# Banded attention's 36 steps dealt out 3, 1, 1 and 2 to a weight slot instead of 2 throughout, and each score matmul waiting for its own PSUM bank alone

## The chip, the cores and the metric

One core of a Trainium2 chip runs the whole program as one launch. The metric is the device time of an execution in microseconds (us), the median of three runs. Five engines work side by side, each through its own list of instructions in order: TensorE (PE in the profile, its weight loads PEld), VectorE (DVE), ScalarE (ACT), GpSimd (POOL) and SyncE (SP), which issues the transfers. They meet at semaphores.

## The reference, cut to what matters

Two transformer blocks over 512 tokens of width 1024, all in float32. The first block projects the normed input by one matrix into the parts of three branches and their gates. The change lies where branch A, attention in a band of 128 positions, runs beside the projections of branch C and of gate A:

```python
qa = apply_rope(rms_norm(qa.reshape(B, S, 8, 64), qn_a[l]), cos, sin)      # 8 query heads, 2 key heads
out_a = window_attention(qa, ka, va, sink_a[l])      # blocks of 128 queries, their own and the neighbouring keys
qc = apply_rope(rms_norm(qc.reshape(B, S, 8, 64), qn_c[l]), cos, sin)
kc = apply_rope(rms_norm(kc.reshape(B, S, 8, 64), kn_c[l]), cos, sin)
out_c = diff_attention(qc, kc, vc, lam)
g = sigmoid(gate_logits)
merged = g[0] * (out_a @ w_oa) + g[1] * (out_b @ w_ob) + g[2] * (out_c @ w_oc)
```

## The kernel before

**Groups and slots.** Every big product is a group (`groups()`): `qc`, `kc`, `vc` are the projections of branch C, `gA0` and `gA1` the two halves of gate A, `bA0` and `bA1` the product of branch A's output with `w_oa`. A group's weights come in slots of 128 x 1024 numbers, two of its eight k-tiles to a slot, so each of `qc`, `kc`, `vc`, `gA0`, `gA1` has four slots. ACT copies a slot into `whi`, and POOL (for `qc`, `kc`, `vc`) or DVE (for the rest) takes the rounding error into `wlo`. TensorE then does four blocks of six matmuls for a slot, one block for each of the PSUM banks 0 to 3. At a group's last slot each block is complete and is read by `evac`.

**Steps beside the slots.** Attention is written as a generator, `window()`, in each engine's program. It has 36 steps, and `Flow.pump` takes one. `slots()` deals the steps out by `rate`: at rate 2 a step stands behind the second and the fourth block of a slot, at rate 3 one behind each of the second, third and fourth, at rate 1 one behind the fourth. A step is pumped at the same place of each engine's program. With u the step's number, TensorE does these things in step u: `turn(u - 3)`, the transposes of a finished softmax into bank 6; for even u `scores(u)`, the scores of heads u and u + 1 into banks 4 and 5; for odd u `values(u - 5)`, two products into bank 7. DVE does `lowest(u)`, which reads the score out of bank 4 + u % 2 into the tile `T8` with its row minimum (L1089), and `shares(u - 1)`, which sums, inverts and scales (L1095, L1097, L1099). ACT copies the transposes out and takes the exponentials. Every eighth step has a block of 128 queries finished: ACT's `high` (L1637) writes `oahi` and DVE's `low` (L1103) `oalo`, which `bA0` multiplies.

**Rotary embedding.** The four blocks of `qc` and of `kc` need more work: a copy and a square on ACT (L1602, L1608), a sum on DVE (L1038), an inverse root on POOL (L2037, L2039), then `products` on DVE (L1043, L1051), `turn` on POOL (L2047, L2048), `sums` on DVE (L1056). `Flow.later` sets these behind a count of slots: `products` of blocks 0 and 1 at the end of the group's last slot; at the end of the next slot their `sums` and the `products` of blocks 2 and 3; one slot later the `sums` of those. `rotary(r, b)` on TensorE transposes block b into bank 4 + b % 2. Blocks 0 and 1 are transposed at the end of the second slot behind the group, just before the step pumped there, blocks 2 and 3 one slot later. They use the banks of the scores, so they wait too until `lowest` has read what the last `scores` wrote there: `free[b]` holds that condition, and `take(b)` waits for it.

Of the kernel before, what the change touches and what calls it, by code (L numbers as in the profile page):

```python
# [151 lines left out]
def build(nc, d, out):  # L152
# [76 lines left out]
    qcT = sb("qcT", AR + 107.5, [128, 4, S])  # L229
    kcT = sb("kcT", AR + 115.5, [128, 4, S])  # L230
    vc = sb("vc", AR + 123.5, [128, 4, 512])
# [144 lines left out]
    def tensor_program(t):  # L376
# [4 lines left out]
        def take(b):  # L381

            for s, n in free[b]:
                w.wait_ge(s, n)

        def mm(o, l, r, first, last):
            return t.matmul(o, l, r, start=first, stop=last)  # L387
# [4 lines left out]
        def group(name, act, ready, freed, rate=1, more=False, beside=None, last=True):  # L392
            first, n_s, n, mode = PLACE[name]
            for s, b, end in slots(flow, name, rate, nothing):
                i, bank = first + s, BANK[name] + b
                h = i % HL
                if b == 0:
                    w.wait_ge(lo_done[h], i // HL + 1)
                if s == 0 and not more:
                    take(bank)  # L400
                if s == 1 and beside:
                    beside(b, bank)
                for kk in range(2):
                    k = 2 * s + kk
                    ready(k, b)
                    ahi, alo = act(k)
                    if mode == "tok":
                        c0, c1 = kk * n, kk * n + n
                        rows = slice(b * 128, b * 128 + 128)
                        o = ps[bank][:, 0:n]  # L410
                        mm(o, ahi[:, rows], whi[h][:, c0:c1], s == 0 and kk == 0 and not more, False)
                        mm(o, ahi[:, rows], wlo[h][:, c0:c1], False, False)
                        op = mm(o, alo[:, rows], whi[h][:, c0:c1], False, last and end and kk == 1)
                    else:
                        c0 = kk * n + b * 128
                        o = ps[bank][:]
                        mm(o, whi[h][:, c0:c0 + 128], ahi, s == 0 and kk == 0 and not more, False)
                        mm(o, whi[h][:, c0:c0 + 128], alo, False, False)
                        op = mm(o, wlo[h][:, c0:c0 + 128], ahi, False, last and end and kk == 1)
                if end:  # L420
                    op.then_inc(blocks, 1)
                    reader = freed(b)
                    free[bank] = [reader] if reader else []
                elif b == (4 if mode == "tok" else n // 128) - 1:
                    op.then_inc(slot_read[h], 1)
# [4 lines left out]
        def h_ready(n):  # L430
            return (lambda k, b: w.wait_ge(e_lo, 8 * n - 8 + k + 1)) if n else (lambda k, b: w.wait_ge(n_lo, k + 1))
# [128 lines left out]
        def rotary_group(name, r, nj, rate=1):  # L560
            def freed(b):
                flow.later(3 + b // 2 if r else 5, lambda: rotary(r, b, nj))
                return r_c, 4 * r + b + 1
            group(name, hT, h_ready(0), freed, rate)

        def window():
            w.wait_ge(r_e, 8)

            def scores(u):

                n, h = w_units[u]
                k0, wd, _ = span_a(n)
                take(4)
                take(5)
                for i in range(2):
                    base = 64 * i
                    mm(ps[4 + i][:, 0:wd], qaT[base:base + 64, h, n * 128:(n + 1) * 128],
                       kaT[base:base + 64, 0, k0 * 128:k0 * 128 + wd], True, True).then_inc(a_qk, 1)
                    free[4 + i] = [(a_mx, u + i + 1)]

            def turn(u):
                wd = span_a(w_units[u][0])[1]
                w.wait_ge(a_nm, 3 * u + 3)
                take(6)
                for k in range(wd // 128):
                    op = across(6, k, T8[u % 4][:, k * 128:(k + 1) * 128])
                op.then_inc(a_tr, 1)
                free[6] = [(a_ev, u + 1)]

            def values(u):  # L590

                n, h = w_units[u]
                k0, wd, _ = span_a(n)
                w.wait_ge(a_ev, u + 2)
                if h == 0:
                    take(7)
                for k in range(wd // 128):
                    for i in range(2):
                        op = mm(ps[7][64 * i:64 * i + 64, h * 128:(h + 1) * 128], va[:, k0 + k, 64 * i:64 * i + 64],
                                PT[(u + i) % 4][:, k * 128:(k + 1) * 128], k == 0, k == wd // 128 - 1)  # L600
                        if k == wd // 128 - 1:
                            op.then_inc(a_pv, 1)
                if h == 3:
                    free[7] = [(oa_lo, n + 1)]

            for u in range(36):
                if 3 <= u < 35:
                    turn(u - 3)
                if u < 32 and u % 2 == 0:
                    scores(u)  # L610
                if u >= 5 and u % 2:
                    values(u - 5)
                yield
# [180 lines left out]
            group("bB%d" % half, lambda k: (obhi[:, k, :], oblo[:, k, :]), lambda k, b: w.wait_ge(ob_lo, 4),  # L794
                  lambda b: (b_v, 4 * half + b + 1), 2)
        flow.beside.append(window())
        rotary_group("qc", 2, 4, 2)
        rotary_group("kc", 3, 4, 2)
        group("vc", hT, h_ready(0), lambda b: (vc_c, b + 1), 2)
        flow.flush()  # L800
        for half in range(2):
            group("gA%d" % half, hT, h_ready(0), lambda b: (g_t, 8 + 4 * half + b + 1), 2)
# [50 lines left out]
    def vector_program(v):  # L853
# [13 lines left out]
        def group(name, evac, rate=1):  # L867
            for _, b, end in slots(flow, name, rate, split):
                if end:
                    evac(b, ps[BANK[name] + b], DONE[name] + b + 1)  # L870
# [160 lines left out]
        def rotary(r, n_heads):  # L1031
            def evac(b, p, done):
                q, wd = 4 * r + b, 64 * n_heads
                r_, q0, q1 = (rk[:, b, :] if r == 1 else raw[b])[:, 0:wd], tp[b % 2][:, 0:wd], tq[b % 2][:, 0:wd]
                s0 = 64 + 16 * b
                ss = st[:, s0:s0 + n_heads]
                w.wait_ge(r_q, q + 1)
                v.tensor_reduce(ss, heads(q0, n_heads), AX.X, ALU.add).then_inc(r_s, 1)  # L1038
                cg = rt[:, 2 * r, b, :].unsqueeze(1).to_broadcast([128, n_heads, 64])

                def scale():
                    w.wait_ge(r_r, 2 * q + 2)
                    v.tensor_tensor(heads(r_, n_heads), heads(r_, n_heads), ss.unsqueeze(2).to_broadcast([128, n_heads, 64]),  # L1043
                                    ALU.mult).then_inc(r_x, 1)

                def times_cos():
                    w.wait_ge(r_x, q + 1)
                    w.wait_ge(r_tab, 13)
                    if b < 2:
                        w.wait_ge(r_s, q + 3)  # L1050
                    v.tensor_tensor(heads(q0, n_heads), heads(r_, n_heads), cg, ALU.mult).then_inc(r_m, 1)  # L1051

                def add():
                    w.wait_ge(r_m, q + 1)
                    w.wait_ge(r_g, q + 1)
                    v.tensor_tensor(r_, q0, q1, ALU.add).then_inc(r_a, 1)  # L1056

                waiting.append((scale, times_cos, add))
                if b % 2:
                    two = tuple(waiting)  # L1060
                    waiting.clear()

                    def products():
                        two[0][0]()
                        two[1][0]()
                        two[0][1]()
                        two[1][1]()

                    def sums():
                        two[0][2]()  # L1070
                        two[1][2]()

                    flow.later(1 + b // 2, products)
                    flow.later(2 + b // 2, sums)
            return evac
# [338 lines left out]
        for half in range(2):  # L1414
            group("bB%d" % half, branch(0, half), 2)
        flow.beside.append(window())
        group("qc", rotary(2, 8), 2)
        group("kc", rotary(3, 8), 2)
        group("vc", none, 2)
        flow.flush()  # L1420
        for half in range(2):
            group("gA%d" % half, none, 2)
# [55 lines left out]
    def scalar_program(a):  # L1478
# [413 lines left out]
        for half in range(2):  # L1892
            group("bB%d" % half, none, 2)
        flow.beside.append(window())
        group("qc", rotary(2, 8, qcT), 2)
        group("kc", rotary(3, 8, kcT), 2)
        group("vc", values, 2)
        flow.flush()
        for half in range(2):
            group("gA%d" % half, gates(1, half), 2)  # L1900
# [45 lines left out]
    def gpsimd_program(g):  # L1946
# [248 lines left out]
        for half in range(2):  # L2195
            group("bB%d" % half, none, 2)
        flow.beside.append(iter(range(36)))
        group("qc", rotary(2, 8), 2)
        group("kc", rotary(3, 8), 2)
        group("vc", none, 2)  # L2200
        flow.flush()
        for half in range(2):
            group("gA%d" % half, none, 2)
# [248 lines left out]
```

## Time and profile before

| | |
|---|---|
| median of 3 runs | 1698.64 us (1698.61 to 1698.65) |
| the profiled execution, its own time | 1700.36 us |
| its span in the trace | 1698.5 us |
| TensorE busy | 1633.2 us, 96% of the span |
| VectorE, ScalarE, GpSimd busy | 883.5, 645.4 and 366.1 us |
| mean granted TensorE clock | 0.991 of full speed |
| the 36 steps and the groups beside them | from 318.24 us to 468.5 us; `bA0` begins at 479.53 us |

The span is shorter than the execution by what lies around it, 1.9 us. A busy TensorE is not one at its peak: the ends of matmuls are modelled, and the distance between two starts tells what one takes.

### The profile page before, as it was taken

What the parts mean: (1) busy time and instruction counts of PE and PEld (TensorE: products, weight loads), DVE (VectorE), ACT (ScalarE), POOL (GpSimd) and SP (SyncE); (2) the same over time, 40 slices, a digit from 0 to 9 for tenths busy, and PEclk for the clock granted to TensorE, in tenths of its full rate; (3) what the DMA queues carried; (4) which work ended last, traced back from release to release, by engine and by line L of the source; (5) the groups of instructions that cost most, each with busy time, mean ns of one, the idle gap of its engine ahead of it and who ended that gap; (6) DMA issues with size and microseconds to landing.
All of it is one profiled execution on the core that took longest, in us unless ns stands there. A gap on an engine that the chain in (4) does not pass through costs nothing.

```text
span 1698.5 us, 19241 instructions
## 1 busy us (share of the span) xinstructions
PE 1633.2 (96%) x7582; PEld 1292.9 (76%) x7582; DVE 883.5 (52%) x1401; ACT 645.4 (38%) x1106; POOL 366.1 (22%) x318
## 2 busy tenths in 40 slices
PE   5999998988999999999999999998999999999998
PEld 3566787766767788888888887775788888888886
DVE  5446555366357555444343324587564767777222
ACT  4332223355445433333322212466563444444222
POOL 3444214364012116111110205033202400000000
PEclk9999998999999999999999999999999999999999
DMA  6121112211221323233333322321102232332322
GB/s 231 51 74 37 50 55 75 87 57 56 75 63 50 112 88 98 92 95 99 99 100 94 94 98 70 112 63 38 44 7 76 86 98 90 97 99 87 124 88 73
DMA packets 39221, 139.51 MB, mean 82 GB/s; under 512 B 4331, under 2 KB 4971, under 8 KB 38940
## 3 DMA queue, kind: packets, MB, share of 16 engines
q1 hardware_dynamic: 39132, 138.29, 25.3%
q8 instruction: 60, 0.98, 0.2%
q14 instruction: 29, 0.24, 0.0%
HBM read 136.14 MB, written 2.10 MB: 81 GB/s over the span
## 4 chain that ended last, share of the span: by engine, by line
PE 83%; DVE 6%; POOL 5%; ACT 3%; issue 3%; DMA 1%; SPq 0%; POOLq 0%; DVEq 0%; ACTq 0%
PE ps L387 80%; PE ps L390 3%; POOL sqs L2105 2%; POOL sqt L2103 1%; DVE raw L1056 1%; ACT whi L1489 1%; DVE W L1307 0%; DVE wlo L863 0%; DVE T L1089 0%; DMA wraw<-in_ws 0%; DMA x<-in_x 0%; POOL Lb L2158 0%; DVE tp L1051 0%; DVE sd L962 0%; DVE raw L1043 0%
## 5 line engine op out<-in xcount | busy, mean ns | idle before, releaser
L863 DVE TENSOR_TENSOR wlo<-wraw,whi 128x1024 fp32r<-128x1024 f32 (+2 forms) x220 | 271.8, 1240 | 442.7 <-ACT whi L1489 442.0
L387 PE MATMUL ps<-hThi,whi 128*128 128x512 f32 x1128 | 455.0, 403 | 1.6 <-DVE skT L1394 0.9
L387 PE MATMUL ps<-hThi,wlo 128*128 128x512 f32 x1128 | 441.5, 391 | 0.0
L387 PE MATMUL ps<-hTlo,whi 128*128 128x512 f32 x1128 | 440.9, 391 | 0.0
L1489 ACT ACTIVATE whi<-wraw 128x1024 fp32r<-128x1024 f32 (+2 forms) x244 | 251.9, 1037 | 481.9 <-PE ps L387 467.9
L387 PEld LDWEIGHTS ps<-hThi,whi 128*128 128x128 f32 x1128 | 212.9, 189 | 57.5 <-issue 16.2
L387 PEld LDWEIGHTS ps<-hTlo,whi 128*128 128x128 f32 x1128 | 213.0, 189 | 45.5 <-issue 3.6
L387 PEld LDWEIGHTS ps<-hThi,wlo 128*128 128x128 f32 x1128 | 212.6, 188 | 45.3
L387 PE MATMUL ps<-whi,hThi 128*128 128x512 f32 (+1 forms) x224 | 90.1, 402 | 6.8 <-DVE wlo L863 6.8
L387 PE MATMUL ps<-whi,hTlo 128*128 128x512 f32 (+1 forms) x224 | 85.9, 383 | 0.0
L387 PE MATMUL ps<-wlo,hThi 128*128 128x512 f32 (+1 forms) x224 | 85.8, 383 | 0.0
L2242 POOL TENSOR_TENSOR small<-small,vec 128x1 f32<-128x1 f32 x4 | 2.2, 540 | 355.0 <-DVE small L1469 355.0
L1956 POOL TENSOR_TENSOR wlo<-wraw,whi 128x1024 fp32r<-128x1024 f32 x24 | 59.1, 2463 | 85.5 <-ACT whi L1489 85.5
L2122 POOL TENSOR_TENSOR ft<-ft,R 128x512 f32<-128x512 f32 x22 | 27.9, 1290 | 199.1 <-ACT ft L1729 199.1
L387 PE MATMUL ps<-whi,achi 128*128 128x512 f32 x176 | 69.2, 393 | 0.0
L387 PE MATMUL ps<-wlo,achi 128*128 128x512 f32 x176 | 68.5, 389 | 0.0
L387 PE MATMUL ps<-whi,aclo 128*128 128x512 f32 x176 | 68.5, 389 | 0.0
L387 PE MATMUL ps<-achi,whi 128*128 128x512 f32 x176 | 68.5, 389 | 0.0
L387 PE MATMUL ps<-aclo,whi 128*128 128x512 f32 x176 | 68.5, 389 | 0.0
L387 PE MATMUL ps<-achi,wlo 128*128 128x512 f32 x176 | 68.5, 389 | 0.0
L387 PEld LDWEIGHTS ps<-whi,hThi 128*128 128x128 f32 x224 | 43.7, 195 | 21.3 <-issue 7.7
L1740 ACT ACTIVATE ft<-vt,vec 128x512 f32<-128x512 f32 x44 | 34.9, 813 | 51.0 <-DVE vt L1245 51.0
(323 smaller groups left out, 2605.7 us busy)
## 6 DMA issues: line engine op xcount, KB each, us to landing
wraw<-in_ws SPq DMA_DIRECT2D x236, 512.0 KB, 3.5
x<-in_x SPq DMA_DIRECT2D x4, 512.0 KB, 7.5
x<-in_x SPq DMA_DIRECT2D x1, 2048.0 KB, 8.4
out<-ys SPq DMA_DIRECT2D x8, 256.0 KB, 2.2
dec<-in_dec SPq DMA_DIRECT2D x1, 1024.0 KB, 15.9
wraw<-in_ws SPq DMA_DIRECT2D x4, 256.0 KB, 2.6
vec<-in_vec SPq DMA_DIRECT2D x1, 788.0 KB, 4.7
w<-in_w SPq DMA_DIRECT2D x1, 512.0 KB, 14.3
```

The source lines that it names most:

```text
L387: return t.matmul(o, l, r, start=first, stop=last)
L390: return t.transpose(ps[b][:, c * 128:(c + 1) * 128], src, ident)
L863: v.tensor_tensor(wlo[h][:, 0:width(i)], wraw[h][:, 0:width(i)], whi[h][:, 0:width(i)].bitcast(F32), ALU.subtract).then_inc(lo_done[h], 1)
L1056: v.tensor_tensor(r_, q0, q1, ALU.add).then_inc(r_a, 1)
L1489: a.activation(whi[h][:, 0:width(i)], wraw[h][:, 0:width(i)], ACT.Copy).then_inc(hi_done[h], 1)
L1740: a.activation(ft[i][:], vt[q % 4][:], ACT.Identity, bias=col("cb2", c), scale=col("cw2", 88 + c)).then_inc(v_a, 1)
L1956: g.tensor_tensor(wlo[h][:, 0:width(i)], wraw[h][:, 0:width(i)], whi[h][:, 0:width(i)].bitcast(F32), ALU.subtract).then_inc(lo_done[h], 1)
L2103: g.tensor_tensor(sqt[:], xT[:, f, :], xT[:, f, :], ALU.mult).then_inc(p_acc, 1)
L2105: g.tensor_tensor(sqs[:], sqs[:], sqt[:], ALU.add).then_inc(p_acc, 1)
L2122: g.tensor_tensor(t[:], t[:], R1[:], ALU.mult).then_inc(u_sr, 1)
L2242: g.tensor_tensor(small[:, 8 + b:9 + b], small[:, 4 + b:5 + b], col("mhalf"), ALU.pow).then_inc(n_rs, 1)
```

## The change

`groups` `qc`, `kc` and `vc` are run at rates 3, 1 and 1 in place of 2, 2 and 2, in the programs of all four compute engines. The gates keep rate 2. So 12, 4 and 4 steps stand beside the three groups where there were 8, 8 and 8, and 16 are left for the 16 places of the two gates, where there were 12. And `scores` no longer waits for both banks before its two matmuls: each matmul waits for its own bank. No instruction is added or removed but waits. The diff; the three hunks left out make the same change of rates in VectorE's, ACT's and POOL's programs:

```diff
@@ -570,10 +570,9 @@
 
                 n, h = w_units[u]
                 k0, wd, _ = span_a(n)
-                take(4)
-                take(5)
                 for i in range(2):
                     base = 64 * i
+                    take(4 + i)
                     mm(ps[4 + i][:, 0:wd], qaT[base:base + 64, h, n * 128:(n + 1) * 128],
                        kaT[base:base + 64, 0, k0 * 128:k0 * 128 + wd], True, True).then_inc(a_qk, 1)
                     free[4 + i] = [(a_mx, u + i + 1)]
@@ -794,9 +793,9 @@
             group("bB%d" % half, lambda k: (obhi[:, k, :], oblo[:, k, :]), lambda k, b: w.wait_ge(ob_lo, 4),
                   lambda b: (b_v, 4 * half + b + 1), 2)
         flow.beside.append(window())
-        rotary_group("qc", 2, 4, 2)
-        rotary_group("kc", 3, 4, 2)
-        group("vc", hT, h_ready(0), lambda b: (vc_c, b + 1), 2)
+        rotary_group("qc", 2, 4, 3)
+        rotary_group("kc", 3, 4, 1)
+        group("vc", hT, h_ready(0), lambda b: (vc_c, b + 1), 1)
         flow.flush()
         for half in range(2):
             group("gA%d" % half, hT, h_ready(0), lambda b: (g_t, 8 + 4 * half + b + 1), 2)
```

The two places that matter below, as the built programs have them. First VectorE behind the end of the group `kc`. `raw` and `tp` are the tiles of the rotary embedding, `T8` those of the attention's scores, `st` holds columns of one number per row. Before:

```order
L1089 ISA T8_0_123,st_132<-ps4,maskA_131,small_61 128x384
L1089 ISA st_132 128x1
L1095 TENSOR_TENSOR st_132<-st_132 128x1
L1097 RECIPROCAL st_132<-st_132 128x1
L1099 TENSOR_SCALAR T8_3_126<-T8_3_126,st_132 128x384
L1056 TENSOR_TENSOR raw0_111<-tp0_116,tp2_118 128x512
L1056 TENSOR_TENSOR raw1_112<-tp1_117,tq1_119 128x512
L1043 TENSOR_TENSOR raw2_113<-raw2_113,st_132 128x512
L1043 TENSOR_TENSOR raw3_114<-raw3_114,st_132 128x512
L1051 TENSOR_TENSOR tp0_116<-raw2_113,rt_110 128x512
L1051 TENSOR_TENSOR tp1_117<-raw3_114,rt_110 128x512
L1089 ISA T8_1_124,st_132<-ps5,maskA_131,small_61 128x384
```

After:

```order
L1088 ISA T8_3_126,st_132<-ps5,maskA_131,small_61 128x384
L1088 ISA st_132 128x1
L1094 TENSOR_TENSOR st_132<-st_132 128x1
L1096 RECIPROCAL st_132<-st_132 128x1
L1098 TENSOR_SCALAR T8_2_125<-T8_2_125,st_132 128x384
L1055 TENSOR_TENSOR raw0_111<-tp0_116,tp2_118 128x512
L1055 TENSOR_TENSOR raw1_112<-tp1_117,tq1_119 128x512
L1042 TENSOR_TENSOR raw2_113<-raw2_113,st_132 128x512
L1042 TENSOR_TENSOR raw3_114<-raw3_114,st_132 128x512
L1050 TENSOR_TENSOR tp0_116<-raw2_113,rt_110 128x512
L1050 TENSOR_TENSOR tp1_117<-raw3_114,rt_110 128x512
L1088 ISA T8_0_123,st_132<-ps4,maskA_131,small_61 128x384
```

Between the `products` of the first two blocks and their `sums` (`raw0`, `raw1`) stands one step less; and the step behind the second `products` is an even one, whose score is in bank 4 (step 16), where it was an odd one with bank 5 (step 17).

Second TensorE where `gA1` ends (`ps3`, the last block) and `bA0` begins (`oahi`, `oalo`). Before:

```order
L387 MATMUL ps3<-hThi_49,wlo0_57 128x512
L387 MATMUL ps3<-hThi_49,whi0_54 128x512
L387 MATMUL ps3<-hTlo_50,whi0_54 128x512
L387 MATMUL ps3<-hThi_49,wlo0_57 128x512
L387 MATMUL ps0<-oahi_136,whi1_55 128x512
L387 MATMUL ps0<-oalo_137,whi1_55 128x512
```

After:

```order
L387 MATMUL ps3<-hThi_49,wlo0_57 128x512
L387 MATMUL ps7<-PT2_129,va_122 64x128
L387 MATMUL ps7<-PT3_130,va_122 64x128
L387 MATMUL ps7<-PT2_129,va_122 64x128
L387 MATMUL ps7<-PT3_130,va_122 64x128
L387 MATMUL ps0<-oahi_136,whi1_55 128x512
L387 MATMUL ps0<-oalo_137,whi1_55 128x512
```

The last `values` of the attention (`PT`, `va`), from which `oahi` and `oalo` are made, moved from eight blocks of matmuls ahead of `bA0` to directly in front of it.

## Rows read from the trace of the kernel before

**Rows 1.** The page's busy times.

```profile
PE 1633.2 (96%) x7582; PEld 1292.9 (76%) x7582; DVE 883.5 (52%) x1401; ACT 645.4 (38%) x1106; POOL 366.1 (22%) x318
```

**Rows 2.** TensorE's waits from 312 to 480 us: total, times, longest.

```profile
PE ps L387 <- DVE st L1089: 7.8, 4, 2.9
PE ps L390 <- DVE st L1089: 2.4, 2, 2.0
```

**Rows 3.** Timeline of TensorE, its waits: start, length, instruction, idle time before it.

```profile
348.03 0.92 PE L387 MATMUL ps<-kaT,qaT 64*128 64x384 f32 x4 [1.43 <-DVE st L1089]
...
358.75 0.92 PE L387 MATMUL ps<-kaT,qaT 64*128 64x384 f32 x4 [2.88 <-DVE st L1089]
...
365.04 0.63 PE L390 MATMUL ps<-vec,raw 128*128 128x128 f32 x4 [0.40 <-DVE st L1089]
...
388.22 0.92 PE L387 MATMUL ps<-kaT,qaT 64*128 64x384 f32 x4 [1.04 <-DVE st L1089]
...
398.91 0.92 PE L387 MATMUL ps<-kaT,qaT 64*128 64x384 f32 x4 [2.40 <-DVE st L1089]
...
405.21 0.63 PE L390 MATMUL ps<-vec,raw 128*128 128x128 f32 x4 [2.03 <-DVE st L1089]
```

**Rows 4.** Timeline of TensorE, work of the steps and blocks.

```profile
382.60 0.49 PE L390 MATMUL ps<-vec,T 128*128 128x128 f32 x3
...
391.93 0.49 PE L390 MATMUL ps<-vec,T 128*128 128x128 f32 x3
392.35 0.88 PE L387 MATMUL ps<-PT,va 128*64 128x128 f32 x12
396.02 0.49 PE L390 MATMUL ps<-vec,T 128*128 128x128 f32 x3
```

**Rows 5.** Timeline of TensorE behind the wait of 2.88 us.

```profile
359.97 0.63 PE L387 MATMUL ps<-wlo,hThi 128*128 128x512 f32 x1
...
363.35 0.39 PE L387 MATMUL ps<-whi,hThi 128*128 128x512 f32 x1
...
364.04 0.60 PE L390 MATMUL ps<-vec,raw 128*128 128x128 f32 x4
```

**Rows 6.** Stretches: length, busy PE, PEld, DVE, ACT, POOL, granted clock, DMA.

```profile
284.00:288.00 4.00, 2.24 (x10) 2.24 (x11) 4.00 (x5) 0.52 (x3) 2.29 (x3) 0.50 0.33 69
288.00:292.00 4.00, 4.00 (x23) 4.00 (x22) 2.39 (x5) 2.43 (x11) 1.75 (x4) 0.55 0.76 217
...
396.00:400.00 4.00, 1.60 (x9) 0.82 (x8) 3.81 (x8) 1.20 (x4) 3.49 (x4) 1.00 0.27 107
```

**Rows 7.** Timeline of VectorE behind the end of `kc`.

```profile
384.44 0.69 DVE L1038 TENSOR_REDUCE st<-tp 128x8 f32<-128x512 f32 x1 [0.46 <-ACT tp L1608]
...
398.15 0.60 DVE L1089 CUSTOM_DVE_ANT_0 T<-ps,maskA,small 128x384 f32<-128x384 f32 x1
...
399.07 0.64 DVE L1099 TENSOR_SCALAR T<-T,st 128x384 f32<-128x384 f32 x1
...
400.76 2.57 DVE L1099 TENSOR_SCALAR T<-T,st 128x384 f32<-128x384 f32 x1
403.25 0.68 DVE L1056 TENSOR_TENSOR raw<-tp,tp 128x512 f32<-128x512 f32 x1
```

**Rows 8.** Timeline of POOL over the same stretch.

```profile
379.87 0.20 POOL L2037 TENSOR_SCALAR st<-st 128x8 f32<-128x8 f32 x1
...
388.39 0.72 POOL L2047 TENSOR_TENSOR tp<-raw,rt 128x256 f32<-128x256 f32 x1
...
400.72 2.39 POOL L1956 TENSOR_TENSOR wlo<-wraw,whi 128x1024 fp32r<-128x1024 f32 x1 [1.22 <-ACT whi L1489]
```

**Rows 9.** Timelines of TensorE, ACT and DVE at the last `values`.

```profile
467.89 0.66 PE L387 MATMUL ps<-PT,va 128*64 128x128 f32 x8
...
468.62 0.60 ACT L1637 ACTIVATE oahi<-ps 128x512 fp32r<-128x512 f32 x1 [2.99 <-PE ps L387]
...
469.25 0.69 DVE L1103 TENSOR_TENSOR oalo<-ps,oahi 128x512 fp32r<-128x512 f32 x1 [5.17 <-ACT oahi L1637]
```

More of the change, by code:

```diff
@@ L1416, in vector_program @@
         flow.beside.append(window())
-        group("qc", rotary(2, 8), 2)
-        group("kc", rotary(3, 8), 2)
-        group("vc", none, 2)
+        group("qc", rotary(2, 8), 3)
+        group("kc", rotary(3, 8), 1)
+        group("vc", none, 1)
         flow.flush()
@@ L1894, in scalar_program @@
         flow.beside.append(window())
-        group("qc", rotary(2, 8, qcT), 2)
-        group("kc", rotary(3, 8, kcT), 2)
-        group("vc", values, 2)
+        group("qc", rotary(2, 8, qcT), 3)
+        group("kc", rotary(3, 8, kcT), 1)
+        group("vc", values, 1)
         flow.flush()
@@ L2197, in gpsimd_program @@
         flow.beside.append(iter(range(36)))
-        group("qc", rotary(2, 8), 2)
-        group("kc", rotary(3, 8), 2)
-        group("vc", none, 2)
+        group("qc", rotary(2, 8), 3)
+        group("kc", rotary(3, 8), 1)
+        group("vc", none, 1)
         flow.flush()
```

## The prediction

> **What bounds the kernel now.** The page's busy times come first: TensorE is busy for 96% of the span [rows 1], so time can only be won where it waits or runs slowly. The list of its waits over the stretch with the attention's steps shows few: four at line 387 and two at line 390, 10.2 us, all for VectorE's line 1089, the read of a score [rows 2]. The timeline places them [rows 3]. They come in two bunches of three, one behind the end of `qc` and one behind the end of `kc`: 1.43, 2.88 and 0.40 us, then 1.04, 2.40 and 2.03 us. In each bunch the first two stand in front of scores and the third in front of the rotary transposes of block 1. So it is not the score reads that are slow, but what VectorE has queued in front of them: the rotary work of the group that has just ended. Nothing else in the 36 steps holds TensorE. After the wait of 2.88 us the clock fell: from 359.97 to 363.35 us the starts of eight matmuls stand 0.42 us apart, behind it 0.23 [rows 5], which is the 1.2 GHz level against 2.4. That lost 8 x 0.19 = 1.5 us, but to no effect, since the transposes of block 1 at 365.04 still had to wait 0.40 us for VectorE. What the present order pays in the two bunches is then 10.2 + 1.5 = 11.7 us.
>
> **The change: how late VectorE is.** I count from the transposes behind the last block of the rotary group, 382.60 us for `kc` [rows 4]. POOL begins the four inverse roots at 379.87 and the rotary products at 388.39, 8.5 us later, and it must do the roots of all four blocks first [rows 8]. VectorE's `sums` and second `products` follow these, and only then, at 398.15, comes the score read, done at 398.8, 16.2 us behind the count [rows 7]. In the new order that same place, behind the second `products`, is held by the read of step 12 (in `kc`'s case 16), in bank 4, as the order of VectorE shows. One step less is queued in between, but POOL's part is what the others wait for, so I do not take the 1.3 us of a step off. On the other side the four blocks of `kc` now follow each other with no step between them, so the group ends about 1.3 us earlier against POOL's `wlo` and roots, and in `qc` a step stands between the third and the fourth block, where VectorE and ACT hand work to each other. Each makes VectorE some 1.3 us later against the end of the group: 17.5 us, between 16.2 and 18.
>
> **When TensorE gets there.** From 388.22 to 396.02 TensorE did scores, 12 matmuls, transposes, values and 12 matmuls, 7.8 us [rows 3, 4]. In the new order there stand between the end of the group and the rotary transposes of blocks 0 and 1: two slots of 24 matmuls, but only two steps. That is the 7.8 us, one more `turn` of 0.42 (391.93 to 392.35 [rows 4]) and 24 more matmuls at 0.23 [rows 5], 5.5 us: 13.7 us. Now the scores no longer wait (their readers are through), and the edit of the banks has nothing left to save there; where it acts it lets one matmul of 0.4 us pass, and I cost it at nothing. The wait moves to the transposes of block 0, which need bank 4, so the read that is done at 17.5: 3.8 us, between 2.5 and 4.3. I take 3.6. Behind them queue the transposes of block 1, the step, and all matmuls of the next slot.
>
> **The second wait.** The transposes of block 1 need bank 5, so the odd step's read. On VectorE one `shares`, the two `sums` and the read itself stand in between. By the rows a `shares` is 0.35 us of small work and its scaling, 0.64 us at 399.07 and 2.57 us at 400.76 [rows 7], where POOL had begun a `wlo` of 2.39 us at 400.72 [rows 8]. ACT casts that slot only after the exponential of the first read, so in the new order, with one `shares` fewer, the scaling should be through before POOL starts. Then 0.35 + 0.4 + 1.2 + 0.6 = 2.55 us, less the 0.46 us of block 0's transposes: 2.1 us. If the scaling falls behind POOL it is 4.3. The Trainium skill says why it can (GPSIMD Engine Reference, Specifications): GpSimd shares its SBUF interface with VectorE and contends with VectorE's two-port and two-input instructions; by that rule the sum is the same, it only names which instructions can be caught.
>
> A bunch then costs 3.6 + 2.1 = 5.7 us and the two 11.4, against 11.7: the main edit wins 0.3 us.
>
> **What is new.** (a) In `qc` three steps stand in a slot, two of the distances being one block (6 x 0.23 = 1.4 us). ACT's part of a step with a raw copy and a square of the rotary group is longer than that, so a turn or a score there waits a little: 0.8 us, between 0 and 1.5. (b) The 36 steps now end in the last slot of `gA1`. In front of `bA0` stand the last `values`, ACT's `oahi` and VectorE's `oalo`. Today these are hidden under eight blocks: `values` begins at 467.89, `oahi` at 468.62, `oalo` at 469.25, for 0.69 us [rows 9]. The chain is 2.05 us, of which TensorE works 0.6: a new wait of 1.5 us, with nothing else for it to do, since `bA0`'s first matmul reads them. (c) The clock. TensorE now stands for 3.6 + 2.1 us with only the 0.5 us of block 0's transposes between. After 2.88 us it lost 1.5; at 1.04 and 2.40 us, a slot apart, the clock stayed full through 396 to 400 [rows 6]; after the longest wait of the kernel it stood at 0.50 and 0.55 for 284 to 292 us, with work in all but 1.8 us of it [rows 6], a loss of about 2.9 us. A low stretch of the length of the first (3.4 us), begun about when the transposes come, lies for 2.1 us in the second wait, where it costs nothing, and then costs 0.6; one as after the long wait costs 2.9. Nearer the first: I take 1.15 us for each bunch, 2.3 in all, between 0 and 5.8. And unlike today nothing stands behind that would have waited anyway.
>
> The Trainium skill has a rule that speaks against this change (TensorE: Matmul & The Clock Gate, HAM oscillation): idle gaps of TensorE let its clock fall to half, and the penalty is half of the time at that clock. By it few long gaps are worse than many short ones of the same sum. The rows agree: 1.5 us lost after 2.88 us of wait, nothing after 2.40.
>
> **The sum.** -0.3 + 0.8 + 1.5 + 2.3 = +4.3 us. The profiled execution took 1700.36 us with a span of 1698.5, so it should become 1704.7, the span 1702.8. The median of the runs, 1698.64, stands 1.7 below the profiled time; the same 4.3 us make it 1702.9 us.
>
> **The rivals.** *The clock holds* (or falls only inside the waits): +2.0 us, 1700.6. For it speaks that two waits of 2.40 and 2.03 us in one bunch cost no clock; against it, that now they stand with no slot between. *The chain of VectorE counts its steps and not POOL's roots.* Then the read of the even step is done one step sooner and not 1.3 us later, at 16.2 - 1.6 = 14.6 us, and the first wait is 0.9 us. A bunch costs 3.0 us, the two 6.0, a gain of 5.7, and with 1.5 for `bA0` and no low clock the kernel is 4.2 us faster: 1694.4. It decides from a first wait below about 2 us on. Against it stand POOL's 8.5 us of roots [rows 8]. *The scaling falls behind POOL's `wlo` in both bunches, with the clock low for longer*: 2.2 us more for each bunch, +8.7 us: 1707.3. *Nothing moves*, as the waits are only placed elsewhere and `bA0` waits for nothing: 1698.6; the rows of the last `values` speak against it.
>
> **How the numbers follow.** Chances: the forecast (a low clock in at least one bunch, both waits as above) 0.55; the clock holds 0.18; the chain by steps, faster, 0.10; caught behind POOL 0.12; nothing moves 0.05. A measurement of this kernel can tell about 0.2% (3.4 us). The forecast's own spread, 1701 to 1705, lies with a quarter of its chance below that bound, so slower by over 0.2% has 0.42 + 0.12 = 0.54, within it 0.13 + 0.18 + 0.05 = 0.36, faster 0.10. The range reaches down to 1698.5, taking in the held clock, and up to 1707: it leaves out the faster case and part of the one behind POOL.
>
> **What would show it.** In the trace of the changed kernel: TensorE's waits at line 387 for the score reads (four, 7.8 us) gone or below 1 us each; at line 390 two pairs of about 3.6 and 2.1 us; a wait of about 1.5 us for `oalo` in front of `bA0`; a granted clock of about half for some us behind each pair. The forecast is wrong if the first wait of a pair is under 2 us, if scores still wait for more than a us each, or if the clock stays full over both.

## The result and the profile after

| | before | after |
|---|---|---|
| median of the five runs of each, taken together | 1698.61 us (1696.29 to 1698.65) | 1706.03 us (1704.13 to 1707.84) |
| ratio | | 1.0047, 95% interval 1.0032 to 1.0061 |
| the profiled execution, its own time and span | 1700.36, 1698.5 us | 1704.13, 1702.2 us |
| first score to the first matmul of `bA0` | 318.24 to 479.53: 161.3 us | 315.11 to 483.50: 168.4 us |

The change costs 7.4 us, or 0.47%. The forecast was +4.3 us; 1706.03 us lies in its range, near the upper end. The profiled execution of after was the fastest of its five, and its span is only 3.7 us longer. It started the attention's steps 3.1 us earlier, though nothing ahead of them was changed. The clock was back earlier in this execution, as the windows behind the kernel's longest wait show for after (columns as in [rows 6]):

```profile
280.00:284.00 4.00, 0.06 (x1) 0.06 (x1) 4.00 (x5) 0.00 (x0) 4.00 (x4) 0.52 0.00 0
284.00:288.00 4.00, 4.00 (x23) 4.00 (x24) 4.00 (x5) 1.79 (x8) 0.47 (x1) 0.63 0.46 142
288.00:292.00 4.00, 4.00 (x29) 3.65 (x28) 1.75 (x8) 3.94 (x11) 3.24 (x8) 1.00 0.71 253
```

In [rows 6] the clock was still at 0.50 and 0.55 in the last two of these stretches, with the same work. So executions of one program can differ by some 3 us here, and the two kernels are compared over the stretch in which they differ: 168.4 against 161.3 us, +7.1, which agrees with the medians.

TensorE's busy time is what it was, 1634.3 us against 1633.2 [rows 1], and so are the other engines':

```profile
PE 1634.3 (96%) x7582; PEld 1292.0 (76%) x7582; DVE 881.6 (52%) x1401; ACT 645.5 (38%) x1106; POOL 367.8 (22%) x318
```

TensorE's waits from 312 to 490 us in after (total, times, longest), the counterpart of [rows 2]:

```profile
PE ps L390 <- DVE st L1088: 11.2, 4, 4.5
PE ps L387 <- DVE oalo L1102: 1.5, 1, 1.5
```

The score matmuls (line 387) no longer wait for the reads; all of it has gone to the rotary transposes (line 390), and `bA0` has a wait of its own. The timeline of TensorE places them:

```profile
361.38 0.63 PE L390 MATMUL ps<-vec,raw 128*128 128x128 f32 x4 [3.08 <-DVE st L1088]
364.07 1.09 PE L390 MATMUL ps<-vec,raw 128*128 128x128 f32 x4 [2.06 <-DVE st L1088]
...
400.08 1.08 PE L390 MATMUL ps<-vec,raw 128*128 128x128 f32 x4 [4.48 <-DVE st L1088]
402.77 1.09 PE L390 MATMUL ps<-vec,raw 128*128 128x128 f32 x4 [1.60 <-DVE st L1088]
...
483.50 0.47 PE L387 MATMUL ps<-oahi,whi 128*128 128x512 f32 x1 [1.54 <-DVE oalo L1102]
```

Two pairs stand where [rows 3] has two bunches of three. With them the clock falls, as the windows of after show (length, busy PE, PEld, DVE, ACT, POOL, granted clock, DMA):

```profile
360.00:364.00 4.00, 0.63 (x4) 0.42 (x4) 3.93 (x11) 2.32 (x5) 2.78 (x4) 0.76 0.00 0
364.00:368.00 4.00, 3.93 (x21) 3.21 (x22) 2.19 (x3) 2.77 (x6) 1.60 (x1) 0.50 0.30 86
368.00:372.00 4.00, 4.00 (x17) 3.25 (x17) 0.00 (x0) 0.04 (x1) 2.39 (x1) 0.89 0.21 65
396.00:400.00 4.00, 0.00 (x0) 0.00 (x0) 4.00 (x7) 0.04 (x1) 3.39 (x4) 0.95 0.39 133
400.00:404.00 4.00, 2.32 (x10) 1.98 (x11) 3.93 (x8) 2.40 (x6) 2.78 (x2) 0.50 0.01 2
404.00:408.00 4.00, 4.00 (x23) 2.99 (x22) 2.11 (x4) 2.70 (x6) 0.29 (x1) 0.69 0.42 131
```

Taken as either full or half, the two levels that the starts of [rows 5] show, 4 us at a mean of 0.76 hold 1.9 us at half; together each pair has 6.8 us at half clock. About 2 us of these TensorE stands, in the other 4.8 it works. By this estimate that costs it 2.4 us a pair, 4.8 in all, against 1.5 before.

**Waits that the list doesn't show.** The two sums above give +2.5 us of waits and +3.3 of clock, 5.8 of 7.1. The rest lies inside three pairs of score matmuls, as the timeline of after shows:

```profile
374.86 1.39 PE L387 MATMUL ps<-kaT,qaT 64*128 64x384 f32 x4
376.18 0.50 PE L387 MATMUL ps<-whi,hThi 128*128 128x512 f32 x1
...
389.01 0.92 PE L387 MATMUL ps<-kaT,qaT 64*128 64x384 f32 x4
```

A pair usually takes 0.85 us up to the next instruction and shows a length of 0.92; this one takes 1.32 and shows 1.39. The same holds at 413.04 (1.32 us) and at 341.67 (1.39 us). Its second matmul waits for bank 5, but the first is still counted as busy, so there is no idle time to list. That is 0.47 + 0.47 + 0.54 = 1.5 us. At 374.86 and 413.04 the bank is being copied out by ACT, behind the transposes of block 3; the timeline of ACT and TensorE in after at the second of them:

```profile
412.38 1.08 ACT L1612 ACTIVATE kcT<-ps 128x512 f32<-128x512 f32 x2 [5.64 <-PE ps L390]
412.62 0.49 PE L390 MATMUL ps<-vec,T 128*128 128x128 f32 x3
413.04 1.39 PE L387 MATMUL ps<-kaT,qaT 64*128 64x384 f32 x4
```

In the order before, the step pumped there was an odd one, without scores.

### The profile page after: what moved, and what is told of

Same layout as the page of the kernel before. It is cut to its first block, busy times and chain, and to the rows that moved or that the text cites. A ratio compares the mean times of both kernels' runs of the same rounds, so it can differ in the third digit from the quotient of the medians.

```text
span 1702.2 us, 19226 instructions
## 1 busy us (share of the span) xinstructions
PE 1634.3 (96%) x7582; PEld 1292.0 (76%) x7582; DVE 881.6 (52%) x1401; ACT 645.5 (38%) x1106; POOL 367.8 (22%) x318
## 4 chain that ended last, share of the span: by engine, by line
PE 83%; POOL 6%; DVE 5%; ACT 3%; issue 3%; DMA 1%; SPq 0%; POOLq 0%; DVEq 0%; ACTq 0%
PE ps L387 80%; PE ps L390 3%; POOL sqs L2104 2%; POOL sqt L2102 1%; ACT whi L1488 1%; POOL st L2038 1%; DVE W L1306 0%; POOL wlo L1955 0%; DVE wlo L862 0%; DMA x<-in_x 0%; POOL Lb L2157 0%; DMA wraw<-in_ws 0%; DVE sd L961 0%; DVE uT L1014 0%; POOL tq L2046 0%
## 6 DMA issues: line engine op xcount, KB each, us to landing
w<-in_w SPq DMA_DIRECT2D x1, 512.0 KB, 13.8
```

## The experiments

Each time stands beside runs of the kernel before on the same chip, whose median was 1697.6 to 1698.0 us. A ratio given can differ by up to 0.0007 from the quotient of the two medians. "The stretch" is the time from the first score to the first matmul of `bA0`.

**banks_only and rates_only: the two halves of the change.** The first is the kernel before with the edit of the banks alone, the second has the rates alone:

```diff
--- rates_only, against the changed kernel
+                take(4)
+                take(5)
                 for i in range(2):
                     base = 64 * i
-                    take(4 + i)
```

> The banks' edit alone, rates 2, 2, 2 kept. Theory A (the waits are those for VectorE's rotary work, and the edit only lets one score matmul of about 0.4 us go ahead of it): 0 to 1 us faster than before, 1698.1 us; the four waits at the scores stay, each up to 0.4 us shorter, and the two at the transposes grow by as much. Rival B (the banks' edit is what moved the waits from the scores to the transposes and cost the time): most of the 7.4 us shows here, 1703 us or more, and no wait at line 387.

> The rates alone (3, 1, 1), both banks waited for before each pair of scores. Theory A: as the whole change or up to 1 us slower, 1706 to 1707 us; two pairs of waits at the transposes of about 3 to 4.5 and 2 us, 1.5 us in front of the first product with branch A's output, low clock behind both pairs. Rival B: near the kernel before, 1699 us.

banks_only took 1698.58 us, ratio 0.9998 (0.9989 to 1.0007): nothing. rates_only took 1707.35 us, 1.0054 (1.0041 to 1.0066), a stretch of 169.1 us: the whole loss comes from the rates. That it is slower than the changed kernel (1.0047) is not shown, as the two intervals overlap. TensorE's waits in rates_only:

```profile
PE ps L390 <- DVE st L1089: 11.2, 4, 4.9
PE ps L387 <- DVE oalo L1103: 1.5, 1, 1.5
PE ps L387 <- DVE st L1089: 0.6, 1, 0.6
PE ps L387 <- ACT qcT L1613: 0.5, 1, 0.5
PE ps L387 <- ACT kcT L1613: 0.5, 1, 0.5
```

The last three are the waits hidden in the changed kernel; where both banks are waited for ahead of the pair they have names. Likewise the score waits of banks_only fell to 4.2 us in three from 7.8 in four [rows 2], with no time won: the edit moves a wait in between the two matmuls and so out of the list.

**early_end: the gates at rates 3 and 2.** The steps end a group of slots earlier, everything else is as changed:

```diff
-            group("gA%d" % half, none, 2)
+            group("gA%d" % half, none, 3 - half)
```

> The whole change, but with rate 3 in the first half of gate A, so that the 36 steps end a slot and a half earlier. Theory A: the wait of 1.54 us for the last part of branch A's output is gone and nothing else changes: 1.5 us below the changed kernel, 1704.5 us. Rival C (that wait only stands in for another that comes next, such as a weight slot's split): no change, 1706 us.

1703.9 us, 1.0036 (1.0022 to 1.005), whose interval overlaps that of the changed kernel. The wait of `bA0` is gone, the four others are 3.08, 1.60, 4.45 and 1.61 us. The stretch is 167.3 us, 1.1 less than in after. That it is not 1.5 less has a reason in the trace: behind `kc` the clock was low for 10.2 us in this execution, where it was 6.8 in after. The term for `bA0` stands: a wait of 1.54 us that goes when the steps end earlier.

**filled: TensorE kept at work.** Added work, 8 matmuls ahead of the rotary transposes of block 0 and 6 ahead of block 1, whose product in bank 6 nobody reads:

```diff
+            if r > 1 and b < 2:
+                take(6)
+                for _ in range(8 if b == 0 else 6):
+                    mm(ps[6][:], hThi[:, 0, 0:128], hThi[:, 0, :], True, True)
             take(bank)
```

> The whole change, with matmuls that nobody reads (8 of 128x512 in front of the transposes of block 0 of qc and kc, 6 in front of those of block 1), written into bank 6 while TensorE would wait; the output is unchanged. Theory A (the clock that falls in the long waits costs some 4.8 us by the profile of the changed kernel, 2.4 behind each pair): the clock stays at full speed, the filling lies inside the waits, and the kernel is 3.5 to 5 us below the changed one, about 1701.5 us, with less spread between runs. Rival D (the clock is a by-product, and the loss comes from the waits alone): 1706 us or up to 3 us more.

1702.41 us, 1.0026 (1.0016 to 1.0037), 3.6 us less than the changed kernel although it does 28 matmuls more. Theory A held, but for one of its two pairs. Behind `qc` the clock stayed full; behind `kc`, where 2.58 us of wait were left, it fell for 3.4 us:

```profile
360.00:364.00 4.00, 2.79 (x15) 1.00 0.22 89
396.00:400.00 4.00, 1.42 (x7) 0.90 0.29 108
400.00:404.00 4.00, 4.00 (x25) 0.67 0.01 2
```

(Columns: length, busy PE, granted clock, DMA.) The stretch is 165.1 us, 3.3 less than in after. The filling only takes the place of waiting, so what it wins is the clock's: 3.4 us at half in place of 13.6, at most 1.7 us lost in place of 4.8.

**vc_one: only `vc` at rate 1**, `qc` and `kc` at 2.

> The kernel before with one edit: vc at rate 1, so rates 2, 2, 1, both banks waited for. Theory A: the bunch behind qc stays as before (1.43, 2.88, 0.40 us), the one behind kc becomes about 2.5 at the scores or transposes and 2.3 at the transposes, and the wait of 1.5 us in front of the products with branch A's output appears, since the steps end in the last slot of gate A; with some low clock 2 to 4 us slower than before, 1701.5 us. Rival E (three steps in a slot of qc are what costs): no slower than before, 1698.6 us.

1701.2 us, 1.0021 (1.0012 to 1.0031). The bunch behind `qc` is that of [rows 3] (1.43, 2.90, 0.42); behind `kc` stand 2.41 and 2.06 us at the transposes, with the clock low for 6.8 us from 398 on, 0.50 us for ACT's copy of `kcT` and 1.54 for `bA0`. With one group changed about half of the loss is there (0.0021 of 0.0047); the other half is then left for the rates of `qc` and `kc`.

**no_roots: POOL's inverse roots taken out.** In `qc` and `kc` the power becomes a multiplication by 1, so the heads are scaled wrongly:

```diff
-                g.tensor_tensor(ss, ms, col("mhalf", 0, n_heads), ALU.pow).then_inc(r_r, 1)
+                if r > 1:
+                    g.tensor_scalar(ss, ms, 1.0, 0.0, ALU.mult, ALU.add).then_inc(r_r, 1)
+                else:
+                    g.tensor_tensor(ss, ms, col("mhalf", 0, n_heads), ALU.pow).then_inc(r_r, 1)
```

> The whole change, but with POOL's inverse roots (128x8, 1.64 us each) of qc and kc replaced by a multiplication by one of about 0.2 us; the rotary norms of branch C are left out by this, so its output is not the reference's. Theory A (POOL's chain of four roots and then the products sets when VectorE can read the score): the chain gets 5.7 us shorter for each group, the first waits (3.1 and 4.5 us) vanish and with them the low clock; 9 to 13 us below the changed kernel, 1695 us. Rival F (VectorE's own queue of rotary work and steps sets it, POOL runs beside): the waits shrink by under 1 us each, 1703 to 1706 us.

1701.72 us, 1.0024 (1.0014 to 1.0035), some 4 us below the changed kernel where theory A said 9 to 13. Its timeline of TensorE:

```profile
362.93 0.63 PE L390 MATMUL ps<-vec,raw 128*128 128x128 f32 x4 [3.03 <-DVE st L1088]
365.61 1.09 PE L390 MATMUL ps<-vec,raw 128*128 128x128 f32 x4 [2.06 <-DVE st L1088]
...
397.26 0.63 PE L390 MATMUL ps<-vec,raw 128*128 128x128 f32 x4 [0.95 <-DVE st L1088]
```

Behind `kc` the first wait fell from 4.48 to 0.95 us: there the roots set the chain, as the prediction said. Behind `qc` it stayed at 3.03. So the roots don't set it there, and the prediction's ground was right in one place of two.

**turn_later: the transposes one slot later.** This tests whether the waits go when TensorE comes to these transposes later. The changed kernel with early_end's rates, and blocks 0 and 1 of `qc` and `kc` are transposed with blocks 2 and 3, at the end of the third slot behind the group (the same edit in ACT's `across`):

```diff
-                flow.later(3 + b // 2 if r else 5, lambda: rotary(r, b, nj))
+                flow.later(4 if r > 1 else 3 + b // 2 if r else 5, lambda: rotary(r, b, nj))
```

> The whole change with rate 3 in the first half of gate A, and all four rotary transposes of qc and of kc at the end of the third slot behind the group (blocks 0 and 1 one slot later than now). Theory A (TensorE meets an unfinished chain only because the transposes of blocks 0 and 1 stand one slot too early): VectorE is through when TensorE arrives; the pairs of 3.1 and 2.1, 4.5 and 1.6 us shrink to about 1 us each bunch, the waits for ACT's copies between transposes of the same bank included, and the clock stays full; 1689 us, 9 us below the kernel before. Rival G (the wait only moves to the next scores, which need the same reads): 1703 us.

1689.64 us, 0.9948 (0.9936 to 0.9961): 8 us faster than the kernel before and 16 faster than the changed one. TensorE's waits from 312 to 471 us, and the stretch as one window (busy PE, granted clock, DMA):

```profile
PE ps L390 <- ACT kcT L1612: 1.7, 1, 1.7
PE ps L390 <- ACT qcT L1612: 0.5, 1, 0.5
```

```profile
317.89:471.04 153.15, 150.90 (x804) 1.00 0.22 69
```

No wait for a score's read is left in the list (the one of 0.54 us inside a pair of scores stays, at 344.46), and the clock never falls.

**before_turn_later: the same edit in the kernel before**, with its rates of 2.

> The kernel before with only the transposes a slot later, rates 2, 2, 2. Theory A: the waits at the scores (7.8 us) stay, those at the transposes (2.4 us) give way to short ones; 1 to 4 us faster than before, 1696 us, so the gain of later transposes needs the new rates. Rival H (the place of the transposes is all that matters): as far below 1698.6 as the version with the new rates, 1690 us.

1695.9 us, 0.9989 (0.998 to 0.9998). The four waits at scores stay (1.43, 2.84, 1.03, 2.46 us), since with rates of 2 the scores themselves come while VectorE is late. The uneven rates and the later transposes only pay together: the rates keep scores out of VectorE's late time, the later transposes keep the banks' other user out of it.

**short_wlo: POOL's `wlo` cut to 64 columns.** In the slots of `qc`, `kc` and `vc` most of the weights' rounding error is left out:

```diff
+                    wd = 64 if i in beside_rotary else width(i)
-                    g.tensor_tensor(wlo[h][:, 0:width(i)], wraw[h][:, 0:width(i)], whi[h][:, 0:width(i)].bitcast(F32),
+                    g.tensor_tensor(wlo[h][:, 0:wd], wraw[h][:, 0:wd], whi[h][:, 0:wd].bitcast(F32),
```

> The changed kernel, but POOL's subtraction into wlo takes only 64 of the 1024 columns for the slots of qc, kc and vc; the rest of each slot's rounding error is left as it stood, so the output is not the reference's. It asks what sets VectorE's lateness behind qc, where leaving out the inverse roots changed nothing. In the changed kernel's trace the second sums (line 1055) takes 2.88 us behind qc and 2.81 us behind kc, beside a wlo of 2.84 us on POOL, against 0.68 us alone. Theory A: this one held-up sums is on the chain in both places, so the first wait of each pair shrinks by 2.2 us: 3.08 to about 0.9, and 4.48 to about 2.3; the second waits stay near 2.06 and 1.60; with shorter waits less of the clock is lost (1 to 3 us), so the kernel takes about 5 us less than the changed one, near 1700. Rival B: the chain is made of hand-overs (ACT's copies, POOL's turn) and the sums would have waited anyway: the first waits stay within 0.3 us of 3.08 and 4.48 and the time near 1705. Between the two: if the chain is held by POOL's turn for one block more, about 1 us of each is won.

1699.43 us, 1.0012 (1.0003 to 1.0021). POOL and VectorE behind `qc`, first in after, then in short_wlo:

```profile
353.84 2.84 POOL L1955 TENSOR_TENSOR wlo<-wraw,whi 128x1024 fp32r<-128x1024 f32 x1
354.36 2.88 DVE L1055 TENSOR_TENSOR raw<-tp,tq 128x512 f32<-128x512 f32 x1
```

```profile
356.31 0.76 POOL L1959 TENSOR_TENSOR wlo<-wraw,whi 128x64 fp32r<-128x64 f32 x1
356.82 0.81 DVE L1058 TENSOR_TENSOR raw<-tp,tq 128x512 f32<-128x512 f32 x1
...
361.80 0.63 PE L393 MATMUL ps<-vec,raw 128*128 128x128 f32 x4 [1.04 <-DVE st L1091]
364.48 0.63 PE L393 MATMUL ps<-vec,raw 128*128 128x128 f32 x4 [2.06 <-DVE st L1091]
```

The first wait fell from 3.08 to 1.04 us by what the `sums` no longer loses, 2.07 us; behind `kc` the waits became 1.27 and 2.06. Theory A holds: behind both groups one `sums`, held for as long as POOL's `wlo` runs, is on the chain. Behind `kc` the first wait lost 3.2 us, a us more than that `sums`. The edit acts there in a second place: in after the four roots start behind a `wlo` of 2.4 us (POOL at 378.39), and here the first `sums` begins 6.9 us behind the last sum of squares in place of 8.0. The Trainium skill says that GpSimd shares its SBUF interface with VectorE and contends with its two-input instructions (GPSIMD Engine Reference, Specifications); the trace agrees, 2.88 against 0.81 us for the same instruction.

**turn_later_both: the edit of the banks where it acts**, turn_later with both banks waited for ahead of the pair.

> The version with the rotary transposes one slot later (1689.6 us), but with scores waiting for both banks ahead of its first matmul as the kernel before does. It asks what the edit of the banks is worth where it acts. In the changed kernel three pairs of score matmuls take 1.39, 1.32 and 1.32 us from their first to the next instruction where the others take 0.85: the second of the pair waits inside it, 1.5 us in all, which the list of waits doesn't show because the first is still counted as running. Theory A: the wait only moves in front of the pair (three waits of about 0.5 us come up in the list), and the first matmul no longer runs under it: 0 to 0.4 us more for each, the kernel 0 to 1.2 us slower, no difference that can be measured. Rival B: the edit removed nearly all of these waits, and without it the kernel becomes 3 us slower or more. Rival C: split pairs cost TensorE time of their own, so waiting for both at once makes it over 1 us faster.

1689.79 us, 0.9956 (0.9942 to 0.9969), against 1689.64 with the edit. Waits of 0.57, 0.45 and 0.45 us came up in front of the three pairs, as theory A said. The edit is worth nothing that can be measured.

## Why the prediction was right in kind and short in size

| term | forecast, us | measured, us |
|---|---|---|
| the bunches of before, with their clock | -11.7 | -11.7 |
| the two pairs of waits | +11.4 | +11.2 |
| small waits | +0.8 | +1.5 |
| the wait of `bA0` | +1.5 | +1.5 |
| half clock while TensorE works | +2.3 | +4.8 (estimate from the windows) |
| sum | +4.3 | +7.3 (stretch +7.1, medians +7.4) |

**The waits.** Moved, not removed: 3.6 and 2.1 us were forecast for each pair, 3.08 and 2.06, 4.48 and 1.60 came. TensorE reached the transposes 13.6 us behind the end of `qc` and 13.8 behind that of `kc` (counted from 344.66 and 381.78), as forecast (13.7). The score's read was through 16.5 us behind the one (361.15) and 18.1 behind the other (399.85), where 17.5 was forecast for both. The first waits so missed in opposite directions, and that the sum of the waits came out within 0.2 us is in part luck. The scaling (line 1098, 0.65 us at 400.23) was through before POOL's `wlo` at 401.88, so the rival in which it is caught fell. In the second pair the wait is 1.60 because block 0's transposes took longer at half clock. filled and turn_later show that these waits and what follows from them are the loss.

**The step that was mis-sized: the clock.** The prediction took 1.15 us for each pair, from a low stretch of 3.4 us [rows 5] of which 2.1 would fall into the second wait. The stretches were 6.8 us long, twice that, and cost about 2.4 us each. Busy time gives nearly the same: without its hidden waits TensorE was busy for 155.63 - 1.48 = 154.2 us of the stretch in after. The window shown for turn_later ends one matmul short of `bA0`; up to `bA0` TensorE was busy for 151.13 us there, without the hidden waits 151.13 - 1.38 = 149.8, with the same instructions at full clock. That is 4.4 us less. The windows of after and before:

```profile
315.11:483.50 168.39, 155.63 (x805) 0.96 0.20 63
```

```profile
318.24:479.53 161.29, 151.12 (x806) 0.99 0.21 66
```

The prediction had the longer case in its hand, the 2.9 us read from [rows 6], and weighed the nearer row. What doubled the stretch is not shown. The second wait, with only 0.5 us of work between, is an obvious candidate: vc_one and no_roots have pairs of that kind too and lose clock in each, turn_later has single waits (0.49, 1.73 us) and loses none. But no_roots has nearly the same pair behind `qc`, 3.03 and 2.06 us, with a low stretch of only 3.4 us, and short_wlo's 1.04 and 2.06 us lose nothing (rows in the last section).

The Trainium skill puts the penalty at half of the time at the low clock (TensorE: Matmul & The Clock Gate, HAM oscillation). The trace agrees: 4.4 us more of busy time for about 9.6 us of work at half clock. The conclusion that the prediction drew from that rule, few long gaps are worse than many short ones, came true in the sum here (13.6 us at half clock with four waits at the transposes, 3.4 with the six waits of before), though not as an order by length: a wait of 2.40 us [rows 3] lost nothing, 1.27 and 2.06 us did.

By the number alone the measured 1706.03 us is nearer to the rival that has the scaling caught behind POOL and the clock low for longer (1707.3) than to the forecast (1702.9). Half of that rival came: the longer low clock, not the caught scaling.

**The small waits** were looked for in `qc` alone. One came there (0.54 us, VectorE's read). Two more came where the prediction had not looked: an even step now stands directly behind the transposes of block 3, and its second score needs the bank that ACT is still copying. This term missed a reader of the bank, not a duration.

**How late VectorE is.** The step "POOL's part is what the others wait for" held for `kc` (no_roots: 4.48 to 0.95 us) and failed for `qc` (3.08 to 3.03). There VectorE's own queue sets the chain: the last sum of squares starts at 347.61, the score's read is through at 361.2, 13.6 us later; in no_roots the two are 349.08 and 362.8, the same distance. Of that 2.1 us are the `sums` caught behind POOL's `wlo`, which the prediction had seen only as a danger for the scaling, not as a part of the chain. The rival that the chain counts VectorE's steps is so half true for `qc`. The queue does hold one step less, worth 1.6 us, but an `oalo` (line 1102, 0.69 us at 352.68) now lies in it. So it became only 0.6 us shorter (14.2 us in before, 344.38 to 358.53), and the first wait did not fall below 2 us.

**The banks** were costed at nothing, and banks_only and turn_later_both show nothing.

## What to carry to other kernels

Dealing out the same work differently doesn't remove a wait as long as the engine that is late stays late: it moves to the next user of the same buffer. Ask who else takes the bank, and move that user too; here the rates alone cost 9 us, the later transposes alone won 2, and both together, with the gates' rates of early_end, won 8. Two waits with little work between them need a wide range for the clock: of the pairs at the transposes, those of filled left aside, one had no low clock, one 3.4 us, most 6.8 and two 10.2. And a wait between two short pipelined matmuls isn't in the list of waits: compare the distance from one start to the next with that of an undisturbed pair.

## What was not expected of the hardware

The same waits did not always cost the same clock. Waits of 1.04 and 2.06 us with one set of transposes between left it full in short_wlo behind `qc`, and 1.27 and 2.06 us behind `kc` of the same execution let it fall:

```profile
364.00:368.00 4.00, 3.52 (x27) 2.90 (x28) 0.99 (x5) 2.70 (x7) 0.08 (x1) 1.00 0.36 131
...
396.00:400.00 4.00, 2.28 (x13) 1.98 (x15) 2.23 (x7) 2.35 (x5) 0.38 (x1) 0.60 0.40 115
400.00:404.00 4.00, 4.00 (x18) 3.04 (x15) 1.22 (x1) 1.69 (x4) 0.00 (x0) 0.55 0.08 26
```

The windows of no_roots behind `qc`, where waits of 3.03 and 2.06 us gave half of the low stretch that 3.08 and 2.06 gave in after:

```profile
364.00:368.00 4.00, 2.39 (x15) 2.09 (x17) 3.75 (x7) 2.35 (x5) 2.42 (x1) 0.64 0.00 0
368.00:372.00 4.00, 4.00 (x22) 3.15 (x19) 0.00 (x0) 1.60 (x4) 2.33 (x1) 0.93 0.40 131
```

(Columns as in [rows 6].) By the windows' means the low stretches beside the attention were 3.4 us long (before, banks_only, before_turn_later, and vc_one behind `qc`, each at the single wait of 2.1 to 2.9 us; no_roots behind `qc`; filled), 6.8 us (both in after; rates_only and early_end behind `qc`; short_wlo, no_roots and vc_one behind `kc`) or 10.2 us (rates_only and early_end behind `kc`). What decides between them was not settled; nor was why executions of one program leave the low clock at 284 to 292 us at different times.

POOL's `wlo` also held VectorE's smallest instructions: in after, a sum of two columns of one number per row (line 1094) took 1.76 us at 402.54 while POOL's `wlo` ran, where the same one took 0.15 us at 399.85. The timeline of POOL and VectorE in after:

```profile
401.88 2.41 POOL L1955 TENSOR_TENSOR wlo<-wraw,whi 128x1024 fp32r<-128x1024 f32 x1 [1.22 <-ACT whi L1488]
402.01 0.61 DVE L1088 CUSTOM_DVE_ANT_0 T<-ps,maskA,small 128x384 f32<-128x384 f32 x1
402.54 1.76 DVE L1094 TENSOR_TENSOR st<-st 128x1 f32<-128x1 f32 x1
```

The read of the score out of PSUM (line 1088), which began while the same `wlo` ran, took its usual 0.61 us.
